# Gates stretched over three steps, a second low part ahead of the inverse root, and first tiles whose low-part products run two blocks behind

## The reference, cut to what matters

```python
def second_block(x, ...):
    for l in range(2):
        mix = hybrid_mixer(x, w_in[l], ...)                # projections of x, mixing, @ w_out
        x = layer_norm(ALPHA * x + mix, ln1_g[l], ln1_b[l])
        f = conv_ffn(x, w_up[l], ffn_conv_w[l], w_down[l])
        x = layer_norm(ALPHA * x + f, ln2_g[l], ln2_b[l])

def conv_ffn(h, w_up, ffn_conv_w, w_down):
    u = h @ w_up                                           # 1024 x 5632
    a, b = u[..., :2816], u[..., 2816:]
    a = causal_dwconv(a, ffn_conv_w)                       # three taps along the tokens
    return (gelu(a) * b) @ w_down                          # 2816 x 1024
```

## Time and profile before

| | us |
|---|---|
| median of three runs | 2472.53 |
| lowest, highest | 2470.16, 2475.63 |
| the profiled execution's own time | 2469.96 |
| its span in the trace | 2468.1 |
| PE busy in the span | 2391.6 (97%), 13253 matmuls |
| DVE busy | 1811.9 (73%) |
| ACT busy | 1305.9 (53%) |

### The profile page before, as it was taken

One profiled execution on the slowest core, in us unless ns is written; L12 is line 12 of the kernel. 1 busy time (PEld: TensorE's weight loads), 2 busy tenths in 40 slices (PEclk: granted clock), 3 DMA queues, 4 the chain that ended last, 5 costly groups with the idle time before them and its releaser, 6 DMA issues.

```text
span 2468.1 us, 33384 instructions
## 1 busy us (share of the span) xinstructions
PE 2391.6 (97%) x13253; PEld 1958.8 (79%) x13253; DVE 1811.9 (73%) x2855; ACT 1305.9 (53%) x1971; POOL 86.2 (3%) x89
## 2 busy tenths in 40 slices
PE   7999899999999998999999999999999999999998
PEld 2575558788776786888888888888898999988998
DVE  6764567677553546999999999999877776677774
ACT  3245332222233445877877778787645554546554
POOL 0000010000010000000000000000000001100002
PEclk8999999999999999999999999999999999999999
DMA  7410045555332114988989889898743445433452
GB/s 294 177 63 35 1 153 192 191 207 189 140 137 86 52 52 175 368 329 331 367 334 366 329 331 362 333 369 332 271 169 122 154 171 205 154 137 137 171 188 103
DMA packets 71651, 510.68 MB, mean 207 GB/s; under 512 B 7905, under 2 KB 9057, under 8 KB 10049
## 3 DMA queue, kind: packets, MB, share of 16 engines
q1 hardware_dynamic: 68690, 500.21, 54.1%
q10 hardware_dynamic: 2208, 6.32, 0.7%
q0 software_dynamic: 592, 1.97, 0.2%
HBM read 506.23 MB, written 2.23 MB: 206 GB/s over the span
## 4 chain that ended last, share of the span: by engine, by line
PE 86%; DVE 8%; ACT 4%; DMA 1%; issue 1%; ACTq 0%; DVEq 0%; SPq 0%
PE bank L815 84%; DVE UL L2205 2%; ACT UH L1685 2%; DMA consts<-in_c 1%; PE bank L1253 1%; PE bank L932 1%; DVE arena L2213 1%; DVE HT L2205 0%; ACT L1688 0%; DVE arena L2978 0%; ACT arena L1688 0%; DVE arena L2205 0%; ACT arena L1931 0%; DVE arena L2209 0%; DVE small L2272 0%
## 5 line engine op out<-in xcount | busy, mean ns | idle before, releaser
L2205 DVE TENSOR_TENSOR UL<-ring,UH 128x1024 fp32r<-128x1024 f32 (+1 forms) x804 | 971.7, 1220 | 307.1 <-ACT UH L1685 288.5
L1685 ACT CAST UH<-ring 128x1024 fp32r<-128x1024 f32 (+1 forms) x804 | 830.4, 1040 | 546.6 <-PE bank L815 515.8
L815 PE MATMUL bank<-XH,UH 128*128 128x256 f32 x1040 | 304.1, 292 | 17.3 <-DVE XL L2213 11.7
L815 PE MATMUL bank<-XL,UH 128*128 128x256 f32 x1040 | 296.5, 285 | 0.0
L815 PE MATMUL bank<-XH,UL 128*128 128x256 f32 x1040 | 296.2, 285 | 0.0
L815 PE MATMUL bank<-UH,HGh 128*128 128x512 f32 (+1 forms) x768 | 291.4, 379 | 3.8 <-issue 2.8
L815 PE MATMUL bank<-UH,HGl 128*128 128x512 f32 (+1 forms) x768 | 287.9, 375 | 0.0
L815 PE MATMUL bank<-UL,HGh 128*128 128x512 f32 (+1 forms) x768 | 287.2, 374 | 0.0
L815 PEld LDWEIGHTS bank<-XH,UH 128*128 128x128 f32 x1040 | 201.5, 194 | 26.9 <-DVE UL L2205 12.9
L2252 DVE CUSTOM_DVE_ANT_0 JUNK<-ring,CROW 128x1024 bf16<-128x1024 f32 x176 | 210.2, 1237 | 14.7 <-ACT CROW L1688 9.5
L815 PEld LDWEIGHTS bank<-XL,UH 128*128 128x128 f32 x1040 | 201.8, 194 | 0.3
(11 more groups left out here) (231 smaller groups left out, 3943.1 us busy)
## 6 DMA issues: line engine op xcount, KB each, us to landing
ring<-in_w SPq DMA_DIRECT2D x477, 1024.0 KB, 4.8
XT<-in_x ACTq DMA_DIRECT2D x2, 1024.0 KB, 12.4
bias_scratch<-BIAS POOLq DMA_DIRECT2D x6, 192.0 KB, 2.1
consts<-in_c ACTq DMA_DIRECT2D x1, 1109.0 KB, 8.3
out_y<-XT ACTq DMA_DIRECT2D x2, 512.0 KB, 3.5
BIAS<-bias_scratch POOLq DMA_DIRECT2D x1, 768.0 KB, 7.1
constd<-in_c ACTq DMA_DIRECT2D x1, 768.0 KB, 4.1
consts<-in_c ACTq DMA_DIRECT2D x1, 512.0 KB, 17.9
```

The lines of the kernel that those rows point to most:

```text
L815: return e.matmul(out, lhsT, rhs, start=start, stop=stop, skip_group_check=True)
L1685: return e.copy(out, in_)
L2205: return e.tensor_tensor(out, a, b, op)
```

## The change

Three edits, all in the second block. No arithmetic, matmul, transfer or buffer is added or taken away; only the order in the queues changes.

1. **Gates over three steps.** The gate's parts become functions (`gelu2`, `high2` on ACT; `product2`, `low2` on DVE). `gate2 m` keeps ACT's copy of `a` and DVE's convolution. Gelu and product move behind the unit splits of step u1 m + 1, the high and low part behind those of step u3 m + 1. For tile 0 they stand in step u3 1 and at the head of `gate2 1`; the last tile does all in its own step.
2. **Second low part ahead of the inverse root.** In DVE's norm the call that makes the second unit low part moves from behind block 1 to before the wait for ACT's inverse root.
3. **Low-part products two blocks behind.** The two `duo` steps of the second block use `low_parts_later`: per block k the four products with XH k as soon as XH k is there, then the two products with XL k - 2.

```diff
+            def low_parts_later(st, dsts, starts, l, what):
+                us = [unit(p[0]) for p in st[2]]
+                for u, _, _ in us:
+                    w.wait_ge(*lo_ready.at(u))
+                for k in range(10):
+                    if k < 8:
+                        w.wait_ge(*act.at("xh", l, what, k))
+                        c = slice(128 * k, 128 * k + 128)
+                        for n_, (u, wh, wl) in enumerate(us):
+                            mm(dsts[n_], wh[:, c], XH[:, k, :], k == 0 and starts[n_], False)
+                            mm(dsts[n_], wl[:, c], XH[:, k, :], False, False)
+                    if k >= 2:
+                        w.wait_ge(*vec.at("xl", l, what, k - 2))
+                        c = slice(128 * (k - 2), 128 * (k - 2) + 128)
+                        for n_, (u, wh, wl) in enumerate(us):
+                            i = mm(dsts[n_], wh[:, c], XL[:, k - 2, :], False, k == 9)
...
# PE, duo "u1" (the projections' duo likewise, with "in")
-                        side_by_side(st, (b[:, 0:256], b[:, 256:512]), (True, False), lambda k: XH[:, k, :],
-                                     lambda k: XL[:, k, :], lambda k: vec.at("xl", l, "mid", k))
+                        low_parts_later(st, (b[:, 0:256], b[:, 256:512]), (True, False), l, "mid")
...
# ACT
+            def gelu2(l, m):
+                w.wait_ge(*vec.at("conv2", l, m))
+                apply(AC_[:, m % 2, :], AC_[:, m % 2, :], ACT.Gelu).then_inc(*act.up(("gelu", l, m)))
+            def high2(l, m):
+                w.wait_ge(*vec.at("g2", l, m))
+                copy(Gh2[:, m, :], AC_[:, m % 2, :]).then_inc(*act.up(("gh2", l, m)))
...
                     split_high(unit(st[2][-1][0])[0], UNITS + 1 if st[1][0] in ("f1", "f3") else UNITS)
+                    if st[1][0] == "u1" and st[1][2] > 1:
+                        gelu2(st[1][1], st[1][2] - 1)
+                    elif st[1][0] == "u3" and st[1][2] == 1:
+                        gelu2(st[1][1], 0)
+                    elif st[1][0] == "u3":
+                        high2(st[1][1], st[1][2] - 1)
...
+                    if m == 1:
+                        high2(l, 0)
                     copy(AP_[:, i, 2:258], b[:, 0:256]).then_inc(*act.up(("a", l, m)))
-                    w.wait_ge(*vec.at("conv2", l, m))
-                    apply(AC_[:, i, :], AC_[:, i, :], ACT.Gelu).then_inc(*act.up(("gelu", l, m)))
-                    w.wait_ge(*vec.at("g2", l, m))
-                    copy(Gh2[:, m, :], AC_[:, i, :]).then_inc(*act.up(("gh2", l, m)))
+                    if m == NF - 1:
+                        gelu2(l, m)
+                        high2(l, m)
...
# DVE: product2 and low2 stand at the same places as gelu2 and high2; in norm():
                 centre(early, 8)
+                if not end:
+                    split_low(W.first["ahead", l, n], 2)
                 w.wait_ge(*act.at("rn", l, n))
...
-                    if k == 1 and not end:
-                        split_low(W.first["ahead", l, n], 2)
```

More of the change, by code:

```diff
@@ L834, in side_by_side @@
                             i.then_inc(*sums.up(("unit", u), st[1][n_]))
+            def low_parts_later(st, dsts, starts, l, what):
[14 more added lines that the diff above has]
+                            i = mm(dsts[n_], wh[:, c], XL[:, k - 2, :], False, k == 9)
+                            if k == 9:
+                                i.then_inc(*sums.up(("unit", u), st[1][n_]))
             def moments(tile, nblk, nt, src):
@@ L1514, in tensor_program @@
                         idle(bs[0], 12)
-                        side_by_side(st, [b[:, 0:256] for b in bs], (True, True), lambda k: XH[:, k, :],
-                                     lambda k: XL[:, k, :], lambda k: vec.at("xl", l, "in", k))
+                        low_parts_later(st, [b[:, 0:256] for b in bs], (True, True), l, "in")
                         give(*st[1])
@@ L2731, in low_parts, with product2, low2 @@
                 tt(XL[:, j, :], X[:, j, xs], XH[:, j, :].bitcast(F32), ALU.subtract).then_inc(*vec.up(("xl",) + nxt + (j,)))
+            def product2(l, m):
+                y = AC_[:, m % 2, :]
+                w.wait_ge(*act.at("gelu", l, m))
+                tt(y, y, psum(("u", l, m))[:, 256:512], ALU.mult).then_inc(*vec.up(("g2", l, m), free=[("u", l, m)]))
+            def low2(l, m):
+                w.wait_ge(*act.at("gh2", l, m))
+                tt(Gl2[:, m, :], AC_[:, m % 2, :], Gh2[:, m, :].bitcast(F32), ALU.subtract).then_inc(*vec.up(("gl2", l, m)))
             def norm(l, n):
@@ L2851, in vector_program @@
                     split_low(unit(st[2][-1][0])[0], UNITS + 1 if st[1][0] in ("f1", "f3") else UNITS)
+                    if st[1][0] == "u1" and st[1][2] > 1:
+                        product2(st[1][1], st[1][2] - 1)
+                    elif st[1][0] == "u3" and st[1][2] == 1:
+                        product2(st[1][1], 0)
+                    elif st[1][0] == "u3":
+                        low2(st[1][1], st[1][2] - 1)
                 elif kind == "ffn_gate":
@@ L3014, in vector_program @@
                     i = m % 2
-                    b = psum(("u", l, m))
                     y = AC_[:, i, :]
+                    if m == 1:
+                        low2(l, 0)
                     w.wait_ge(*act.at("a", l, m))
@@ L3022, in vector_program @@
                             ALU.add).then_inc(*vec.up(("conv2", l, m)))
[L3023 to L3026, removed]
+                    if m == NF - 1:
+                        product2(l, m)
+                        low2(l, m)
         def gpsimd_program(e):
```

## The result

The changed kernel takes **2451.81 us** (median of 6 runs, 2450.39 to 2460.16), the kernel before, on the same chip, 2473.94 (6 runs, 2467.74 to 2475.82). The ratio is 0.9924 with a 95% interval of 0.9906 to 0.9942: 14.3 to 23.3 us less. The forecast was 2456, in a range from 2451 to 2463, so the time lies in the range, 0.8 above its lower end.

The account below looks back on a forecast made before the run. PE holds 86% of the chain, but an ACT and DVE round of 6.0 us paces the up stage. Saving 12.5 there plus 3.7 at the starts, 16.2, from 2472.53 gives 2456 us, range 2451 to 2463.

Parts of the forecast that it names:

- up stages, both layers: Up stages: stretched gates let PE start matmuls every 0.12 us, saving 6.25 us per layer, 12.5 in two.
- start and duo, norm 0 layer 0: Behind norm 0 of layer 0: earlier PE start saves at least 1.5 and at most 2.3 us, taken as 1.9.
- norm 1: Behind norm 1 of layer 0: PE starts its duo from XH 0, 0.5 us earlier.
- start and duo, norm 0 layer 1: Behind norm 0 of layer 1: unit 3 could begin at 2265.5 instead of 2266.8, saving 1.3 us.
- The ring: Up stage: ACT and DVE take turns in a 6.0 us round, longer than PE's 5.76, and set the pace.
- The bank: Rival, up stage: the 0.24 us per pair is PE's own bank change; 6.6 us saved, 2466; chance 0.06.
- The starts: Behind the norms: PE starts 1.5 us earlier at both norms 0, 0.5 at norm 1; idle 2.6 and 2.9.
- The cap: Behind norm 0 of layer 0: ACT's eight passes, cast, UL and handoff before unit 3 limit the gain to 2.3 us.
- The clock: Behind the norms: low-clock stretch taken as long as now; if gone altogether, the starts give 4.1 us instead of 3.7.
- The base: Whole kernel: the saving is taken from the three-run median, 2472.53 - 16.2 = 2456.3, not from the profiled execution's 2469.96.
- What would show it: Traces: pairs 5.76 us apart, first step 0.12, UL ready 2 us ahead, no DVE wait before u1 3, shorter idle.
- ping-pong: Rival, up stage: cut gates make DVE and ACT wait alternately, round 8.0 us, 2552; sign DVE idle over 1.1; chance 0.03.

Follow-up runs that it names:

- gates_only: The changed kernel with the duos and the second low part put back as before; 2456.45 us against 2467.76 for the kernel before, ratio 0.9949.
- after_gelu_twice: The changed kernel with each Gelu of the up stage applied twice; 2451.29 us, ratio 0.9916 to the kernel before.
- after_again: The changed kernel unaltered, measured again beside the kernel before; 2451.67 us against 2469.2, ratio 0.9925.
- the second comparison: The changed kernel, unaltered, measured again against the kernel before; 2451.67 us against 2469.2, ratio 0.9925.
- high_first_only: The kernel before with only the duos changed to high parts first, the second low part left in place; 2475.68 us beside 2470.89.
- before_gelu_twice: The kernel before with each Gelu of the up stage applied twice; 2488.95 us, ratio 1.0079 to the kernel before.

## Why the prediction was right

The sum was 16.2; the tail of the profiled pair gave 16.6. That the two agree to 0.4 is in part luck: one term was 0.8 too small, and two were 0.2 and 0.15 too large. Term by term:

| term | predicted | measured |
|---|---|---|
| up stages, both layers | 12.5 | 12.3 (6.16 + 6.13, from gates_only) |
| start and duo, norm 0 layer 0 | 1.9 (1.5 to 2.3) | 2.7 |
| norm 1 | 0.5 | 0.52 |
| start and duo, norm 0 layer 1 | 1.3 | 1.15 |

- **The ring.** Right in cause and size. A pair that is read by starts is 5.99 before and 5.76 after, the lost time was PE's wait for a UL, and lengthening or shortening the ring moved the pair as a ring does (+0.45 for +0.45 above 5.76, nothing below). The 12.5 was 0.2 too high. That the chain of waits didn't name DVE at the borders was a matter of size only: a wait of 0.24 hides in the 0.28 for which the last matmul counts as busy; when it was 0.68 (6.44 - 5.76) the profile reported 0.46.
- **The bank.** The rival with the Trainium skill's rule on its side (TensorE: Matmul & The Clock Gate, "A second HAM failure mode: psum-queue depth-cycling") doesn't hold here. Pairs change banks every 48 matmuls in the changed kernel with a step of 0.12 at the border, and the granted clock of the up stage reads 1.00 (columns as in the earlier trace rows):

```profile
1925.00:2046.00 121.00, 121.00 (x1011) 121.00 (x1010) 91.70 (x148) 65.86 (x107) 0.00 (x0) 1.00 0.50 179
```

The earlier trace rows had already shown the step.
- **The starts.** 1.50 and 0.52, where 1.5 and 0.5 were worked out, and the idle times were to be 2.6 and 2.9: they are 2.62 and 2.97. At norm 0 of layer 1 the stretch ahead gives 1.28; it scatters by 0.2 among kernels with the same code there (before 137.77, gates_only 137.97; after 136.49, after_gelu_twice 136.29), and behind the start 0.13 is lost, since this duo was slow (7.33 against 7.19).
- **The cap.** Mis-sized: that norm 0 of layer 0 can win at most 2.3. It won 1.50 at the start and 1.19 behind it. Two numbers of the step were off. I read unit 2's start in the kernel before off the end of ACT's wait; by PE's starts it is 8.33 behind the duo's first matmul, not 8.15, and unit 3 is 11.21 behind it, not 11.05. And I added passes, cast, UL and hand-off by their full lengths, to 10.25. The passes ended where I had them (7.68 behind the duo's start, 7.70 reckoned), but from there each row begins some 0.1 before the one ahead of it ends, as the cast at 1918.45 against the passes' end at 1918.54, so unit 3 began at +9.93. The cap, taken at unit 3's start, is 2.8, and this duo reached it. Not foreseen either: at that clock unit 2 waits 0.32 for its own UL, which DVE makes behind XL 7.
- **The clock.** The prediction took the slow stretch to be as long as now, and set the case where it goes against the cap. What happened was a mix: gone in layer 0, there in layer 1. That it was gone in layer 0 was luck, but worth little: in after_again it was there, and the up stage is only 0.17 longer (136.45, unit 3 at 10.19 behind the duo's start against 9.93), since the cap takes the rest. That term came out above 1.9 even so, because the slow stretch behind 2.6 of idle time was shorter than before (duo 7.31 against 8.33). The Trainium skill's rule on short idle gaps (the same page, "Why this matters for your kernels") is partly borne out: with 4.1 of idle time the duo was slow in 8 of 8 cases, with 2.6 in 7 of 10, with the gap filled in 0 of 6; the 15 duos behind 2.97 to 3.49 were all slow. By the 2.6 alone the clock can't be counted on.
- **The base.** 2456.3 came from the median of three runs less 16.2, and 2451.8 was measured. The saving is right to 0.4 by the traces; the other 4 lie in the base. By the medians the saving was 22.1 here and 17.5 in the second comparison, so that 2451.8 fell inside the range at all is owed in part to the room left for scatter. The prediction noted that the profiled execution was 2.6 below the median and that nothing it sees varies; from that execution, 2453.8, it would have been nearer.
- **What would show it.** All of it was there: pairs 5.76 apart, UL ready 2.6 us early (1978.74 for a unit that starts at about 1981.4), no wait ahead of u1 3, `a` and convolution close together, idle 2.62 and 2.97. One sign of being wrong came true all the same: DVE idles 0.59 and 0.74 in a pair, 1.33 together, where over 1.1 was to mean ping-pong. The parts don't ping-pong, since both waits go back to PE and the pair takes 5.76. The bound was too tight: of a pair of 5.76 the prediction's own 4.7 us of DVE work leave 1.06 idle, and the 4.7 adds up full lengths, while the rows overlap. The windows over one pair, first of the changed kernel, then of the kernel before (columns as above), have DVE busy for 4.35 and 4.44 us:

```profile
1975.60:1981.36 5.76, 5.76 (x50) 5.76 (x49) 4.35 (x8) 3.10 (x5) 0.00 (x0) 1.00 0.52 183
```

```profile
2000.38:2006.37 5.99, 5.99 (x48) 5.82 (x49) 4.44 (x8) 3.09 (x5) 0.00 (x0) 1.00 0.54 175
```

So by the windows the kernel before idled more (1.55 against 1.41), and the bound could not have told the two apart.

The chain behind it in one piece: the gate of a tile was one chain of six pieces over two engines, and while it ran neither could prepare weights. Stretched over three steps, each piece runs while the other engine splits. The round falls from 6.0 to what PE needs, and 19 waits a layer, each too short to stand in a table of waits, are gone.

## What to carry to other kernels

When two in-order engines hand work to each other and both feed a third, add up the round, hand-offs and all, and hold it against the third one's step; if it is longer by a few per cent, interleave the hand-offs with independent work instead of making any piece faster. Read the bounding engine by starts, not by busy shares, since a wait shorter than an instruction's tail shows in no table of waits. And where two causes cap the same start, undo both in one experiment as well as each alone: here each alone gave about nothing, and both gave 2.6 us.

## What the runs showed of the hardware

**The head scatters.** The stretch ahead of the first duo is the same code in all the kernels, and it took 1773.8 to 1784.2 us in 13 profiled executions. That is as much as half the gain by the medians. The windows from 900 us to the first duo (bounds, length, busy time by engine, then PEclk, DMA, GB/s), first of high_first_only, then of before:

```profile
900.00:1784.00 884.00, 867.73 (x4266) 716.70 (x4266) 778.30 (x850) 647.12 (x742) 6.80 (x8) 0.98 0.84 321
```

```profile
900.00:1776.00 876.00, 860.01 (x4252) 710.12 (x4251) 775.98 (x842) 646.00 (x740) 6.79 (x8) 0.99 0.85 324
```

PE's busy time is 7.7 longer in the one, in a window that is 8.0 longer, and the granted clock reads 0.98 against 0.99; DMA moves the same. Over the whole head it is the same: in the shortest, of before_gelu_twice, PE is busy for 1729.8 us of 1773.7, in the longest for 1741.4 of 1784.1, so that it stands 43.9 and 42.7 us. So the scatter is in how fast PE runs, and goes with its clock; what sets it these runs leave open. It is large enough to account for two comparisons of the same kernels that gave 22.1 and 17.5, while the tails agree to 0.1 (674.8, 674.9). For a change that is confined to a part of the program, the length of that part in the traces is a finer measure than the median.

**The clock behind a short gap is not settled by the gap.** 2.62 us of idle time ahead of the same duo left the clock at 1.00 in three cases and lowered it in seven. Nor does the low level always begin with the duo. In the kernel before, behind 4.12, starts are 0.21 apart from 1913.30 to 1918.63. Behind norm 0 of layer 0 in after_again, they are 0.12 apart from 1915.99 to 1917.06, then about 0.21 until 1920.41, then 0.12 again. It cost 1.0 there, and up to 2.0 behind 4.1 us (8.33 against 6.32).
